# The memory branch of a 1,024-token block: its inputs fetched earlier, its norm beside the last queries, its keys and values at the head of the next stage

## The chip, the core and the metric

One Trainium2 chip, and one of its eight cores. The core has TensorE (PE in the profile; its weight loads are PEld), VectorE (DVE), ScalarE (ACT), GpSimd (POOL) and SyncE (SP), which here only issues transfers. They run side by side and wait for each other through semaphores. The metric is the device time of one execution of the whole program, in microseconds (us).

## What is computed

Two transformer blocks over 1,024 tokens of width 1,024, in fp32. The change touches one part of the first block, the cross attention over a memory of 256 rows:

```python
def _memory_cross_attention(h, mem_n, w_q, w_kv, w_o):
    q = (h @ w_q).reshape(b, s, MEM_HEADS, MEM_HEAD_DIM)                  # 4 heads of 128
    kv = (mem_n @ w_kv).reshape(b, n_mem, 2, MEM_HEADS, MEM_HEAD_DIM)     # 256 rows
    k, v = kv[:, :, 0], kv[:, :, 1]
    sc = jnp.einsum('bshd,bmhd->bhsm', q, k) * MEM_HEAD_DIM ** -0.5
    p = jax.nn.softmax(sc, axis=-1)
    o = jnp.einsum('bhsm,bmhd->bshd', p, v).reshape(b, s, MEM_WIDTH)
    return o @ w_o
```

`h` is the RMS norm of the residual `x` after the first attention has been merged into it, and `mem_n` is the RMS norm of the 256 memory rows with the gain `norm_mem_g`. Nothing else in the program depends on the memory.

## The kernel before

A stage is a Python function that opens a block: each engine gets its own stream of instructions in the order written, and all engines meet at the block's end. Inside it only semaphores order the engines. A tile is 128 tokens; there are eight (ST). A product that matters for precision runs as three fp32r products of a high and a low part (`add_product`, L201 to L203); the memory's keys and values and the scores are plain fp32, each of whose products stands as two records in the trace.

`memory_mixer` (L2240) runs these stages one after the other:

1. `mixed_queries` (L1637) merges the attention output into the residual and makes the queries. Eight chunks of `w_out` are split into the pair `mix_ws` (2 x 4 MB), the weights of `out_rows`. For each tile i the PE does `out_rows(i)` with the previous tile's `turn_out` (eight transposes) in it, then `query(i - 1)`; `turn_query` (four transposes) trails by two. ACT and DVE norm the new residual rows (`norm_out`, `high_out`, `low_out`). The eighth `out_rows` counts `products` to 8, and from there `mix_ws` is read by no one. The queries end up in `qt` (`mem_q`).
2. `load_rows` fetches `mem` (1 MB).
3. `norm_turn` squares the two memory tiles (one on ACT, one on DVE), forms the scale, scales both (ACT), transposes each (PE, eight transposes) and applies the gain column by column (DVE) into `mem_t`.
4. `project_rows` makes the four key heads `km` from four 512 KB loads, two buffers deep.
5. `project_tokens` makes the values `vm` from one 2 MB load.
6. `memory_tiles` (L1974) loads and splits `w_mem_o`, then per tile: `score`, `shift` (row maximum and subtraction, DVE), `exponentials` (ACT), `weigh` (DVE), `turn_probs`, `copy_probs` (ACT), `multiply` by `vm`, `head_high` and `head_low`, and `out_rows` with the pair `cross_ws`. On the PE the order is `score(i)`, `turn_probs(i-1)`, `multiply(i-1)`, `out_rows(i-1)`. A later norm's rows go through `gained` (POOL) to DRAM.

The expert stages follow; they read what `memory_tiles` leaves.

## Time and profile before

| | |
|---|---|
| median of 3 runs | 3433.58 us (3427.8 to 3451.54) |
| the profiled execution, device time | 3434.03 us |
| its span, first to last instruction | 3432.3 us |
| mean granted TensorE clock | 0.958 of full |
| PE busy | 3159.5 us (92%) |
| DVE, ACT, POOL busy | 1610.4, 1411.0, 422.2 us |
| mem_q complete (end of `mixed_queries`) | 754.03 us |
| first `cross_scores` product | 815.82 us |
| third tile's first `cross_scores` product | 839.89 us |

All times below are microseconds from the span's start. A row of the timeline is: start, duration, engine, line, operation, output<-input, shape, how many records (x), and in brackets how long the engine had been idle before it and what released it. A row of a stretch is: from:to, its length, then busy time and number of records (x) of PE, PEld, DVE, ACT and POOL, the granted TensorE clock (PEclk, as a share of 2.4 GHz), the mean busy share of the 16 DMA engines, and GB/s. SPq is a transfer issued by SP; DMA to landing counts from the issue until the data are there.

### The profile page before, as it was taken

What the parts mean: (1) busy time and instruction counts of PE and PEld (TensorE: products, weight loads), DVE (VectorE), ACT (ScalarE), POOL (GpSimd) and SP (SyncE); (2) the same over time, 40 slices, a digit from 0 to 9 for tenths busy, and PEclk for the clock granted to TensorE, in tenths of its full rate; (3) what the DMA queues carried; (4) which work ended last, traced back from release to release, by engine and by line L of the source; (5) the groups of instructions that cost most, each with busy time, mean ns of one, the idle gap of its engine ahead of it and who ended that gap; (6) DMA issues with size and microseconds to landing.
All of it is one profiled execution on the core that took longest, in us unless ns stands there. A gap on an engine that the chain in (4) does not pass through costs nothing. (4 is left out here: it accounts for less than half of the span.)

```text
span 3432.3 us, 39469 instructions
## 1 busy us (share of the span) xinstructions
PE 3159.5 (92%) x15067; PEld 2509.9 (73%) x15067; DVE 1610.4 (47%) x2295; ACT 1411.0 (41%) x2238; POOL 422.2 (12%) x433
## 2 busy tenths in 40 slices
PE   6998998977959999958998999999989889999999
PEld 5767997765847776757776877777777678888787
DVE  4336887323655656552321222332266476565343
ACT  4325777422436666643522333333353333232111
POOL 0001110000122222110000000000000032221332
PEclk9999999998969999979999999999999999999999
DMA  2344231102157777651233222232264222222531
GB/s 86 85 131 112 57 84 60 57 26 81 44 199 285 282 283 272 229 184 44 81 105 102 62 68 68 62 121 83 62 222 137 93 68 82 84 85 82 205 105 53
DMA packets 243195, 397.23 MB, mean 116 GB/s; under 512 B 43575, under 2 KB 162430, under 8 KB 230722
## 3 DMA queue, kind: packets, MB, share of 16 engines
q1 hardware_dynamic: 218386, 346.96, 31.5%
q10 hardware_dynamic: 9072, 30.94, 2.2%
q0 software_dynamic: 15552, 16.82, 1.7%
q8 instruction: 122, 2.00, 0.2%
q14 instruction: 63, 0.52, 0.0%
HBM read 362.41 MB, written 95.65 MB: 133 GB/s over the span
## 5 line engine op out<-in xcount | busy, mean ns | idle before, releaser
L2644 DVE TENSOR_TENSOR moe_wgu_low<-moe_raw,moe_wgu_high 128x2048 fp32r<-128x2048 f32 x94 | 211.2, 2288 | 182.7 <-ACT moe_wgu_high L2601 182.7
L201 PE MATMUL ga_gate<-second_h_high,ga_ws_high 128*128 128x512 f32 x512 | 232.4, 454 | 0.0
L202 PE MATMUL ga_gate<-second_h_low,ga_ws_high 128*128 128x512 f32 x512 | 205.4, 401 | 0.0
L203 PE MATMUL ga_gate<-second_h_high,ga_ws_low 128*128 128x512 f32 x512 | 205.0, 400 | 0.0
L2601 ACT ACTIVATE moe_wgu_high<-moe_raw 128x2048 fp32r<-128x2048 f32 x94 | 174.5, 1906 | 24.3 <-PEq L2275 24.3
L2569 PE MATMUL moe_down<-moe_raw_down,moe_ht 128*128 128x512 f32 x376 | 169.2, 593 | 1.7 <-ACT moe_ht L2634 1.7
L201 PE MATMUL pr_acc<-second_h_high,pr_ws_high 128*128 128x512 f32 x352 | 147.6, 419 | 18.6 <-DVE pr_stage L2946 9.5
L3585 ACT ACTIVATE ga_row<-ga_turned 128x256 f32<-128x256 f32 (+4 forms) x96 | 44.6, 464 | 274.8 <-PE ga_turned L3499 274.8
L201 PE MATMUL moe_up<-moe_wgu_high,moe_xt_high 128*128 128x512 f32 x376 | 152.5, 405 | 4.2 <-DVE moe_xt_low L2650 4.2
L201 PE MATMUL up_bank<-second_h_high,up_w_high 128*128 128x512 f32 x352 | 139.1, 395 | 18.2 <-DVE up_w_low L3180 16.2
L4451 DVE TENSOR_TENSOR second_h_low<-down_hidden,second_h_high 128x1024 fp32r<-128x1024 f32 x42 | 84.7, 2017 | 138.5 <-ACT second_h_high L4426 138.5
L203 PE MATMUL moe_up<-moe_wgu_high,moe_xt_low 128*128 128x512 f32 x376 | 148.5, 395 | 0.0
L202 PE MATMUL moe_up<-moe_wgu_low,moe_xt_high 128*128 128x512 f32 x376 | 148.4, 395 | 0.0
L201 PE MATMUL down_acc<-second_h_high 128*128 128x512 f32 x352 | 138.3, 393 | 7.4 <-DVE second_h_low L4451 7.4
L202 PE MATMUL pr_acc<-second_h_low,pr_ws_high 128*128 128x512 f32 x352 | 141.2, 401 | 0.0
L3489 PE MATMUL ga_scores<-X 64*128 64x256 f32 (+6 forms) x320 | 125.5, 490 | 16.9 <-DMA X<-scratch_fox_k 10.8
L203 PE MATMUL pr_acc<-second_h_high,pr_ws_low 128*128 128x512 f32 x352 | 140.9, 400 | 0.0
L202 PE MATMUL up_bank<-second_h_low,up_w_high 128*128 128x512 f32 x352 | 138.3, 393 | 0.0
L203 PE MATMUL up_bank<-second_h_high,up_w_low 128*128 128x512 f32 x352 | 138.1, 392 | 0.0
L202 PE MATMUL down_acc<-second_h_low,second_h_high 128*128 128x512 f32 x352 | 138.0, 392 | 0.0
L203 PE MATMUL down_acc<-second_h_high,second_h_low 128*128 128x512 f32 x352 | 137.9, 392 | 0.0
L201 PEld LDWEIGHTS ga_gate<-second_h_high,ga_ws_high 128*128 128x128 f32 x512 | 98.6, 193 | 52.9 <-issue 35.1
(581 smaller groups left out, 7833.9 us busy)
## 6 DMA issues: line engine op xcount, KB each, us to landing
moe_raw<-in_w_expert_gate_dram SPq DMA_DIRECT2D x32, 1024.0 KB, 8.5
moe_raw<-in_w_expert_up_dram SPq DMA_DIRECT2D x32, 1024.0 KB, 7.9
moe_raw_down<-in_w_expert_down_dram SPq DMA_DIRECT2D x32, 1024.0 KB, 7.4
scratch_expert_rows<-moe_y ACTq DMA_DIRECT2D x47, 512.0 KB
ga_w<-in_w_in_dram SPq DMA_DIRECT2D x32, 512.0 KB, 4.1
scratch_gates<-ga_stage SPq DMA_DIRECT2D x64, 256.0 KB, 3.6
mb_spare<-scratch_gates SPq DMA_DIRECT2D x32, 512.0 KB, 3.6
up_raw<-in_w_gate_dram SPq DMA_DIRECT2D x22, 512.0 KB, 4.2
```

Source lines behind the costliest of these rows:

```text
L201: nc.tensor.matmul(out, w[0], x[0], start=start, stop=False)
L202: nc.tensor.matmul(out, w[0], x[1], start=False, stop=False)
L203: return nc.tensor.matmul(out, w[1], x[0], start=False, stop=stop)
L2569: last = nc.tensor.matmul(down[:, h * HALF:(h + 1) * HALF], ht[:, c, :], w[:, c, h * HALF:(h + 1) * HALF], start=(c == 0), stop=(c == 1))
L2601: nc.scalar.activation(wgu[i % 2][0][:, :, m, :], raw[(2 * i + m) % RAW][:].rearrange("p (c n) -> p c n", n=FF), ACT.Copy).then_inc(up_hig ...
L2644: nc.vector.tensor_tensor(wgu[i % 2][1][:, :, m, :], raw[(2 * i + m) % RAW][:].rearrange("p (c n) -> p c n", n=FF), wgu[i % 2][0][:, :, m, ...
L3489: last = nc.tensor.matmul(scores[:, at:to], own[0:rows, t * P:(t + 1) * P], other[0:rows, key + at:key + to], start=True, stop=True)
L3585: nc.scalar.activation(pt[:, 0:chunks_of(n), :], turned[:, 0:chunks_of(n), :], ACT.Copy).then_inc(copied, 1)
L4451: nc.vector.tensor_tensor(h_pair[j % 3][1], hidden_of(j), h_pair[j % 3][0], ALU.subtract).then_inc(lows, 1)
```

## The change

The stages 2 to 5 are gone. Their work moves into the two that stay.

- **Space.** The pair `mix_ws` is opened and closed ahead of two tensors `mem_kv` and `mem_rest` of 4 MB each, so that these take its place. `mem_kv` holds `w_mem_kv`; `mem_rest` holds `mem` (1 MB) and `w_mem_o` (2 MB). `mem_t` lies in `gained`.
- **Fetch.** SP, behind its loads of `x`, waits for the eighth `out_rows` (`products` at 8) and then issues `mem`, the four 1 MB parts of `w_mem_kv`, and `w_mem_o`.
- **Norm.** `memory_means` and `memory_gain` (DVE), `memory_scales` (ACT) and `turn_memory` (PE) stand in `mixed_queries` around the last tile's queries. Both memory tiles go through one PSUM tile, `turned_in`, where there were two before.
- **Keys and values.** They open the next stage: `memory_keys` (four heads side by side over the eight chunks), the first tile's `score(0)`, then `memory_values`. ACT copies the keys out in four pieces and the values in one; `score(0)` waits for the keys, `multiply` for the values.

```diff
--- before.py
+++ after.py
-def mixed_queries(k, qt, w, factor, gain):
+def memory_views(W):
+    kv, rest = W
+    return kv, rest[:, 0:2, :], rest[:, 2:6, :]
+
+def mixed_queries(k, qt, mem_t, W, memory, w, factor, gain):
...
+            def turn_memory(t):
+                pe.wait_ge(k.memory_steps["scales"], t + 1)
+                pe.wait_ge(lows_in, ST)
+                if t:
+                    pe.wait_ge(k.memory_steps["gained"], t)
+                for c in range(KD):
+                    last = nc.tensor.transpose(turned_in[:, c, :], rows[t][:, c * P:(c + 1) * P], k.ident[:])
+                last.then_inc(k.memory_steps["turns"], 1)
+
             turn_in(0)
             for i in range(ST + 2):
+                if i == ST + 1:
+                    turn_memory(0)
...
                 if 1 <= i <= ST:
                     query(i - 1)
+            turn_memory(1)
...
+            def memory_scales():
+                step = k.memory_steps
+                act.wait_ge(k.memory_in, 16)
+                act.wait_ge(squares_out, ST)
+                nc.scalar.activation(junk[:], mem[:, 0, :], ACT.Square, accum_out=mem_stats[:, 0, 0:1]).then_inc(step["squares"], 1)
+                act.wait_ge(step["means"], 1)
+                nc.scalar.activation(mem_stats[:, 2, :], mem_stats[:, 1, :], ACT.Sqrt).then_inc(step["roots"], 1)
+                act.wait_ge(step["rstds"], 1)
+                act.wait_ge(turns_in, ST)
+                for t in range(2):
+                    nc.scalar.activation(rows[t][:], mem[:, t, :], ACT.Copy, scale=mem_stats[:, 3, t:t + 1]).then_inc(step["scales"], 1)
...
+                if i == ST + 1:
+                    memory_scales()
                 if i >= 2:
                     query_rows(i - 2)
                     query_cols(i - 2)
...
+            memory_means()
+            memory_gain(0)
+            memory_gain(1)
...
+            sp.wait_ge(products, ST)
+            sp.dma_start(mem, k.dram["mem"].rearrange("a (t p) d -> p (a t) d", p=P)).then_inc(k.memory_in, 16)
+            kv_view = k.dram["w_mem_kv"][0].rearrange("(c p) n -> p c n", p=P)
+            for n in range(4):
+                sp.dma_start(kv[:, 2 * n:2 * n + 2, :], kv_view[:, 2 * n:2 * n + 2, :]).then_inc(k.memory_kv_in[n], 16)
+            sp.dma_start(mem_out, k.dram["w_mem_o"][0].rearrange("(h p) n -> p h n", p=P)).then_inc(k.memory_out_in, 16)
...
+            def memory_keys():
+                pe.wait_ge(k.memory_steps["gained"], 2)
+                for c in range(KD):
+                    pe.wait_ge(k.memory_kv_in[c // 2], 16)
+                    for h in range(MEM_HEADS):
+                        last = nc.tensor.matmul(keys[h], kv[:, c, h * MEM_HD:(h + 1) * MEM_HD], mem_t[:, c, :],
+                                                start=(c == 0), stop=(c == KD - 1))
+                last.then_inc(k_products, 1)
+
+            def memory_values():
+                for c in range(KD):
+                    for t in range(2):
+                        last = nc.tensor.matmul(acc[:, t * MEM_W:(t + 1) * MEM_W], mem_t[:, c, t * P:(t + 1) * P], kv[:, c, MEM_W:],
+                                                start=(c == 0), stop=(c == KD - 1))
+                last.then_inc(v_products, 1)
+
             def score(t):
                 pe.wait_ge(shifted, t)
+                if t == 0:
+                    pe.wait_ge(k_copied, MEM_HEADS)
...
-            for i in range(ST + 3):
+            memory_keys()
+            score(0)
+            memory_values()
+            for i in range(1, ST + 3):
...
+            act.wait_ge(k_products, 1)
+            for h in range(MEM_HEADS):
+                nc.scalar.activation(km[:, h, :], keys[h], ACT.Copy).then_inc(k_copied, 1)
...
                     for c in range(MEM_HEADS):
                         weight(c)
+                    act.wait_ge(v_products, 1)
+                    nc.scalar.activation(vm[:, :, :].rearrange("p c n -> p (c n)"), acc[:], ACT.Copy).then_inc(v_copied, 1)
...
-        with ExitStack() as inner:
-            mem = k.sb("mem_x", [P, MEM_T // P, D], ctx=inner)
-            mem_t = k.sb("mem_t", [P, KD, MEM_T], ctx=inner)
-            load_rows(k, k.dram["mem"].rearrange("a (t p) d -> p (a t) d", p=P), mem)
-            norm_turn(k, "mem_norm", mem, MEM_T // P, k.gain("norm_mem_g"), mem_t)
-            w_kv = k.dram["w_mem_kv"][0]
-            project_rows(k, "mem_k", w_kv[:, 0:MEM_W], MEM_HEADS, mem_t, KD, (km,), tokens=MEM_T)
-            project_tokens(k, "mem_v", [(w_kv[:, MEM_W:].rearrange("(c p) n -> p c n", p=P), 0, MEM_W)],
-                           MEM_W, mem_t, KD, vm, tiles=MEM_T // P)
-        memory_tiles(k, qt, km, vm, logits)
```

On the PE, from the last queries of `mixed_queries` to the first tile of `memory_tiles`, the program had this order (`mix_q_turned` are the last query transposes):

```order
L203 MATMUL mix_q_acc<-mix_wq_high,mix_out_low 128x512
L1744 MATMUL mix_q_turned<-ident,mix_q 128x128 x4
...
L453 MATMUL mem_norm_turned<-ident,mem_norm_scaled 128x128 x16
...
L200 MATMUL mem_k_acc<-mem_t,mem_k_w 128x256 x8
...
L678 MATMUL mem_v_acc<-mem_v_w,mem_v_tokens 128x512 x16
...
L2050 MATMUL cross_scores<-mem_k,mem_q 128x256 x8
```

and has this one after it (`mix_turned_in` now also holds the memory's transposes; `cross_gained` is `mem_t`):

```order
L208 MATMUL mix_q_acc<-mix_wq_high,mix_out_low 128x512
L1750 MATMUL mix_turned_in<-ident,mix_rows 128x128 x8
L1741 MATMUL mix_q_turned<-ident,mix_q 128x128 x4
L1750 MATMUL mix_turned_in<-ident,mix_rows 128x128 x8
...
L2118 MATMUL cross_turned<-cross_gained,mem_kv 128x256 x2
L2118 MATMUL cross_scores<-cross_gained,mem_kv 128x256 x2
...
L2134 MATMUL cross_scores<-mem_k,mem_q 128x256 x4
L2125 MATMUL cross_acc<-mem_kv,cross_gained 128x512 x16
L2134 MATMUL cross_scores<-mem_k,mem_q 128x256 x4
```

The first memory tile's transposes now stand ahead of the last four query transposes, and the 16 value products stand between the first and the second tile's scores. On ACT the memory's square, root and two scalings come ahead of the last query rows, and the key copies open the next stage:

```order
L1841 ACTIVATE mix_junk,mem_stats<-mem_rest 128x1024
L1843 ACTIVATE mem_stats<-mem_stats 128x2
L1847 ACTIVATE mix_rows<-mem_rest,mem_stats 128x1024 x2
L1829 ACTIVATE mix_q<-mix_q_acc 128x512
L1835 ACTIVATE mem_q<-mix_q_turned 128x4x128
...
L2239 ACTIVATE mem_k<-cross_turned 128x256 x2
L2239 ACTIVATE mem_k<-cross_scores 128x256 x2
L2228 ACT_TABLE_LOAD
L2228 ACTIVATE cross_p<-cross_p 128x1024
L2205 ACTIVATE cross_ws_high<-mem_rest 128x1024 x4
L2255 ACTIVATE mem_v<-cross_acc 128x1024
```

So the last query rows wait on ACT behind four new activations, and the value copy stands behind the splitting of `w_mem_o`.

## Rows read from the trace of the kernel before

**Rows 1.** Stretches of 20 us around the memory's stages.
```profile
740.00:760.00 20.00, 9.65 (x48) 7.25 (x46) 1.23 (x1) 3.96 (x6) 0.00 (x0) 0.88 0.16 53
760.00:780.00 20.00, 10.73 (x42) 9.28 (x43) 4.02 (x6) 3.92 (x6) 0.00 (x0) 0.60 0.21 58
780.00:800.00 20.00, 10.24 (x42) 7.78 (x41) 0.00 (x0) 3.15 (x5) 0.00 (x0) 0.82 0.47 153
...
820.00:840.00 20.00, 15.04 (x57) 11.86 (x58) 13.05 (x14) 7.53 (x8) 0.00 (x0) 0.74 0.28 87
```

**Rows 2.** Timeline, the end of `mixed_queries`.
```profile
736.33 1.22 DVE L1907 TENSOR_TENSOR X<-X,mix_acc 128x1024 f32<-128x1024 f32 x1 [3.18 <-PE mix_acc L203]
...
742.91 1.04 PE L1728 MATMUL mix_turned_out<-ident,mix_scaled 128*128 128x128 f32 x8
...
745.04 1.23 DVE L1920 TENSOR_TENSOR mix_out_low<-mix_turned_out,mix_out_high 128x1024 fp32r<-128x1024 f32 x1 [5.68 <-ACT mix_out_high L1814]
...
751.66 0.39 PE L203 MATMUL mix_q_acc<-mix_wq_high,mix_out_low 128*128 128x512 f32 x1
...
753.43 0.60 ACT L1826 ACTIVATE mem_q<-mix_q_turned 128x512 f32<-128x512 f32 x1 [0.75 <-PE mix_q_turned L1744]
```

**Rows 3.** Timeline, load and norm of the memory rows.
```profile
754.28 0.39 SPq L2267 DMA_DIRECT2D mem_x<-in_mem_dram  x1
760.12 1.22 DVE L375 CUSTOM_DVE_ANT_0 mem_norm_junk<-mem_x 128x1024 f32<-128x1024 f32 x1 [13.86 <-PEq L2261]
...
762.11 2.19 ACT L359 ACTIVATE mem_norm_scaled<-mem_x,rstd 128x1024 f32<-128x1024 f32 x2 [0.32 <-DVE rstd L383]
...
767.02 1.23 DVE L390 TENSOR_TENSOR mem_t<-mem_norm_turned,gains 128x1024 f32<-128x1024 f32 x1 [0.48 <-PE mem_norm_turned L453]
```

**Rows 4.** Timeline, the keys and the values.
```profile
772.94 8.59 PE L200 MATMUL mem_k_acc<-mem_t,mem_k_w 128*128 128x256 f32 x32 [5.96 <-DMA mem_k_w<-in_w_mem_kv_dram]
778.22 0.38 ACT L580 ACTIVATE mem_k<-mem_k_acc 128x256 f32 x1 [13.93 <-PE mem_k_acc L200]
...
786.17 0.38 ACT L580 ACTIVATE mem_k<-mem_k_acc 128x256 f32 x1 [4.10 <-PE mem_k_acc L200]
789.63 0.38 ACT L580 ACTIVATE mem_k<-mem_k_acc 128x256 f32 x1 [3.07 <-PE mem_k_acc L200]
...
798.46 16.30 PE L678 MATMUL mem_v_acc<-mem_v_w,mem_v_tokens 128*128 128x512 f32 x32 [8.97 <-DMA mem_v_w<-in_w_mem_kv_dram]
807.94 0.69 DVE L688 COPY mem_v<-mem_v_acc 128x512 f32<-128x512 f32 x1 [39.69 <-PE mem_v_acc L678]
814.80 0.69 DVE L688 COPY mem_v<-mem_v_acc 128x512 f32<-128x512 f32 x1 [6.17 <-PE mem_v_acc L678]
```

**Rows 5.** Timeline of `memory_tiles`: first scores, first two `out_rows`, next scores.
```profile
815.82 1.96 PE L2050 MATMUL cross_scores<-mem_k,mem_q 128*128 128x256 f32 x8 [1.05 <-PEq L634]
...
831.71 0.79 PE L201 MATMUL cross_acc<-cross_ws_high,cross_mixed_high 128*128 128x512 f32 x1 [3.27 <-DVE cross_mixed_low L2195]
...
839.89 1.89 PE L2050 MATMUL cross_scores<-mem_k,mem_q 128*128 128x256 f32 x8
...
847.23 0.50 PE L201 MATMUL cross_acc<-cross_ws_high,cross_mixed_high 128*128 128x512 f32 x1 [1.41 <-DVE cross_mixed_low L2195]
...
852.82 1.89 PE L2050 MATMUL cross_scores<-mem_k,mem_q 128*128 128x256 f32 x8
```

**Rows 6.** Stretches of 2 us: the clock around two pauses and among later transposes.
```profile
744.00:746.00 2.00, 0.00 (x0) 0.00 (x0) 0.96 (x1) 1.00 (x1) 0.00 (x0) 1.00 0.01 4
...
754.00:756.00 2.00, 0.00 (x0) 0.00 (x0) 0.00 (x0) 0.03 (x1) 0.00 (x0) 0.84 0.38 43
...
972.00:974.00 2.00, 2.00 (x12) 2.00 (x11) 0.39 (x2) 0.00 (x0) 0.00 (x0) 0.50 0.00 0
```

**Rows 7.** A 2 us stretch in a burst of nine 1 MB loads.
```profile
954.00:956.00 2.00, 0.00 (x0) 0.00 (x0) 1.79 (x8) 0.21 (x1) 0.00 (x0) 0.50 1.00 426
```

**Rows 8.** Landings of the six `moe_raw` loads among those nine.
```profile
DMA to landing us min/median/max: 5.9/9.9/17.5
```

95 lines of the change are left out of this document (62 added, 33 removed).

## The prediction

> **What bounds the kernel now.** I read the page first: PE is busy 92% of the span, so only places where PE stands still or runs slowly have time to give. The 20 us stretches around the memory's stages show such a place [rows 1]: between 740 and 800 PE is busy for 9.65, 10.73 and 10.24 us of each 20, and the granted clock falls to 0.60 of full. The timeline says what stands there. The last query product ends at 751.66 + 0.39 = 752.05 and the queries are complete at 753.43 + 0.60 = 754.03 [rows 2]. Then `mem` is fetched with nothing else running (issued 754.28, used 760.12) and normed until 767.02 + 1.23 = 768.25 [rows 3]; PE waits 5.96 us for the first key weights and 8.97 us for the value weights [rows 4]; the first scores come at 815.82 [rows 5]. DVE and ACT are nearly idle there [rows 1]. The stretch is a chain: load, norm, load, product, load, product, each alone, with four stage changes between.
>
> The first tile of `memory_tiles` is slow as well: from its `out_rows` at 831.71 to the third tile's scores at 839.89 PE takes 8.18 us, where the second tile takes 852.82 - 847.23 = 5.59 [rows 5]; the clock averages 0.74 in that stretch [rows 1].
>
> **The sum.** I lay the new order along PE with durations from these rows, up to the third tile's scores (839.89 before). Behind them the two programs have the same instructions and waits, so a shift there is carried to the end.
>
> *Fetch.* SP waits for the eighth `out_rows`, which DVE's addition at 736.33 shows as done [rows 2]. All its earlier loads were issued by then (the last `x` tile long before), so nothing is queued ahead. `mem` took 5.84 us from issue to use [rows 3]; in a burst of nine 1 MB loads the earliest landed after 5.9 [rows 8]. So it is there by 736.4 + 5.9 = 742.3. The 16 DMA engines moved 426 GB/s in that burst [rows 7]; `mem` and `w_mem_kv` are 5.24 MB, 12.3 us, so with some 2 us to start the last key weights are there by 751. `w_mem_o` (2.1 MB, 5 us) follows by 756 and isn't asked for before the first scores are through. No other load runs in this time. The transfers cost nothing, and cover is left: the keys want them at 756.9.
>
> *Norm.* DVE's `low_out` ends at 745.04 + 1.23 = 746.27, and ACT is free from 745.0, when `mix_out_high`, which released it, was done [rows 2]. Before, from the start of the DVE square to the end of the first scaling it took 762.11 + 1.1 - 760.12 = 3.1 us, and 4.2 to the second [rows 3]. The same steps here run from 746.3 to 749.4 and 750.5, all under the last query's products, which end at 752.05. The last query rows on ACT, queued behind them, want their product at 752.05 and so lose nothing.
>
> *What stays exposed of it.* `turned_in` is one PSUM tile, so the two memory tiles alternate between PE and DVE. Eight transposes take 1.04 us [rows 2], a gain 1.23 [rows 3]. First transposes 751.9 to 752.95; gain to 754.2; second transposes to 755.3; gain to 756.55. The query transposes and their copy fall between (before, done at 754.03; now some 0.2 later). So the stage ends 2.5 us later than before. A stage change costs 815.82 - (814.80 + 0.69) = 0.33 us [rows 4, 5]. Keys start at 756.9.
>
> *Keys.* Sixteen records at full clock take 789.63 - 786.17 = 3.46 us [rows 4]. There are 64 (32 products): 13.8, and 0.4 until the copy can start: 771.1. Four copies of 0.38 [rows 4] on the path: 772.7.
>
> *score(0)*: 852.82 and 839.89 are starts of such a group; its eight records take 1.7 us at full clock (the group lasts 1.89 with its tail) [rows 5]: 774.4.
>
> *Values*: 32 records, sixteen in 814.80 - 807.94 = 6.86 us [rows 4]: 13.7, to 788.1. Under them lies what used to stand alone in the first tile: the row maximum, the exponentials with their table load, their sum, and the splitting of `w_mem_o`. Before, all of the first tile between its scores and its `out_rows` took 831.71 - 817.78 = 13.9 us, transposes, `multiply` and second scores included [rows 5]; the part that has to be done by 788.1 is shorter than that and has 13.7. The value copy on ACT (1,024 columns out of PSUM, about 1.1 us) runs while PE does score(1).
>
> *First tile.* From a tile's scores to its `out_rows` the second tile took 847.23 - 839.89 = 7.34 us [rows 5]; the same chain stands here: 788.1 + 7.34 = 795.5. `out_rows` at full clock, 5.59: 801.1.
>
> The third tile's scores start at 801.1 in place of 839.89: 38.8 us earlier. The profiled execution took 3434.03, so 3395.2; the median of the runs shown is 0.45 lower: **3394.8, say 3395 us**.
>
> PE's products are the same as before (64 + 32 records of keys and values); what goes is waiting and slow clock. By place: the keys start 772.94 - 756.9 = 16.0 earlier; from there to the last key copy 790.0 - 772.9 = 17.1 becomes 15.8 (1.3); from there to the values 798.46 - 790.0 = 8.4 becomes score(0), 1.7 (6.7); the values 815.8 - 798.5 = 17.4 with a stage change become 13.7 (3.7); the first tile up to its `out_rows` 15.9 becomes 7.3 (8.6); the `out_rows` 8.2 becomes 5.6 (2.6). Sum 38.9, the last digit being rounding.
>
> **The clock.** The forecast takes the high level (2.4 GHz) throughout from 756.9. PE's products pause from 752.05 to 756.9, with 20 transposes in the pause. In the trace products also paused, at least from 742.91 to 746.3, with the eight transposes of 742.91 and four query transposes in the pause, and the clock was 1.00 in 744 to 746 [rows 2, 6]. Behind 752.05, with only four transposes in the pause, it fell: 0.84 on average in 754 to 756 [rows 6]. The new pause is of the first kind. Starting at the low level costs, by rows: the first sixteen key records took 778.22 - 772.94 = 5.28 where 3.46 + 0.4 is full, 1.4 more; the value products took 16.30 where 13.7 is full, 2.6 more [rows 4]; 8.18 against 5.59, again 2.6 [rows 5]. So 1.4 to 2.6 each time the clock has fallen.
>
> The Trainium skill speaks against me here (TensorE: Matmul & The Clock Gate, Part 4: PE-mode transpose): transposes are said not to count as PE work for the clock. By it the new pause is an idle one, the keys would open at 1.2 GHz, and the sum would be that of the first rival. The trace bears it out for the pause behind 752.05 and not for the one before 746.3.
>
> **Rivals.**
> 1. *The clock falls in the pause before the keys, or in the one before the first `out_rows`.* For: it fell behind 752.05, and at 831.71 the first `out_rows` ran slow. Against: the pause at 744, and that the first tile's gaps are now as short as the second tile's (1.41 us before 847.23 [rows 5]), where nothing slowed. Time: 3394.8 + 1.4 to 2.6 = 3396 to 3397.5; both, up to 3400.
> 2. *`mem` lands with the burst behind it.* ACT is in order, so the last query rows would wait behind the memory's square. With `mem` at 751 in place of 742.3 the norm starts 4.7 us later than 746.3, of which 2.4 reach the path (the last product hides the rest), and a longer pause loses the clock too: 38.8 - 2.4 - 2 = 34.4, 3399. Against: the 5.9 of [rows 8].
> 3. *The change doesn't do what it says: the fetch is served only when the stage ends.* Then `mem` is used at 760.1 as before, the norm's alternation ends about 7.7 us after that, and the keys start at 768 at the low clock: 11 + 2 us given back, 3408. Against: `mem` itself was in use 5.84 us after its issue [rows 3], and this issue waits only for a count that is complete at 736.3.
> 4. *Slower than before: the low level stays.* In 972 to 974 PE was busy all of the 2 us and the clock still 0.50 [rows 6]. If it fell at 755 and stayed low through the keys, the values and the first tile, the 39.5 us of full-speed work between 756.9 and 801.1 (13.8 + 1.7 + 13.7 + 7.3 + 5.6, less gaps of 2.6) would double and eat the whole gain; each further tile at the low level, with about 13 us between tiles (852.82 - 839.89 [rows 5]), adds up to 12 and gives 3446. It decides from the end of the first `out_rows` on. Against: in the key and value products the clock came back within their first 16 records each time [rows 4].
>
> **How the numbers follow.** Forecast 0.62; rival 1 0.25; rival 2 0.05; rival 3 0.04; rival 4 0.01; the rest for drift between runs. Low end: the fastest run shown, 3427.8, less 38.8 is 3389; a stage change or pause that is shorter by half a us: 3388. High end: rivals 1 and 2 and the unequal runs, 3405; rival 3 is left out. What a measurement of this kernel can tell from no change is about 1%, 34.3 us, so 3399.2 is the border; forecast and most of rival 1 lie below. Faster by over 1% 0.75, within 1% 0.23, slower 0.02.
>
> **What would show it.** In the profile of the changed kernel: `mem_rest` loaded at 736.4 and used by DVE at 746.3 (rival 2: after 750); the last gain ending near 756.6; the first `cross_turned` product near 756.9 with PEclk 1.00 around it (rival 1: 0.50); key copies near 771.1; values from 774.4 to 788.1; `out_rows` at 795.5; third scores at 801.1. The forecast is wrong if PE waits for a `w_mem_kv` load, if DVE or ACT reaches the first tile's work later than the values' end, or if stages behind 940 lose time that they did not lose before.

## The result, and the profile after

The changed kernel takes 3389.48 us (median of 4 runs, 3387.41 to 3390.73) beside 3434.72 for the kernel before on the same chip: a ratio of 0.9861, 95% interval 0.9825 to 0.9897. Two later comparisons of the same two programs gave 0.9891 (0.9876 to 0.9906) and 0.9889 (0.9873 to 0.9906). The forecast of 3395 us is a ratio of 0.9887 to the 3433.58 us that the prediction started from, and its low end of 3388 one of 0.9867. The 3389.48 us as they stand are inside the range, but they were timed beside a kernel before at 3434.72; put on the prediction's 3433.58 by the ratio they are 3385.9. So the first comparison lies below the forecast range, and the other two are at the forecast.

To read where the time went I cut each profile at two events that all the kernels share. The **first part** runs from the start to the last addition of `mixed_queries` (the row `X<-X,mix_acc`, 736.33 before [rows 2]). The **middle part** runs from there to the third tile's first `cross_scores` (839.89 before [rows 5]). The **last part** is the rest.

| profiled execution | first | middle | last | span |
|---|---|---|---|---|
| before | 736.3 | 103.6 | 2592.4 | 3432.3 |
| changed | 740.8 | 66.3 | 2578.5 | 3385.7 |

The middle part is the change: 37.3 us shorter, where the forecast had 38.8. The 20 us stretches of the changed kernel that answer to [rows 1] show it (columns as there). TensorE is now busy for 16 to 19 of each 20 us, and the 16 DMA engines are nearly full in the first of them (share 0.93).

```profile
740.00:760.00 20.00, 16.46 (x76) 13.06 (x74) 5.15 (x9) 9.18 (x14) 0.00 (x0) 0.91 0.93 360
760.00:780.00 20.00, 16.41 (x78) 14.13 (x79) 1.54 (x2) 2.65 (x6) 0.00 (x0) 1.00 0.18 43
780.00:800.00 20.00, 18.89 (x68) 10.63 (x66) 12.06 (x11) 6.89 (x7) 0.00 (x0) 1.00 0.00 0
800.00:820.00 20.00, 16.06 (x82) 13.32 (x81) 11.62 (x13) 9.18 (x11) 2.42 (x1) 1.00 0.00 1
```

The timeline of the changed kernel, first DVE and SP from the last addition on, then ACT. It answers to [rows 2, 3].

```profile
740.84 0.39 SPq L2014 DMA_DIRECT2D mem_rest<-in_mem_dram  x1
740.84 1.22 DVE L1930 TENSOR_TENSOR X<-X,mix_acc 128x1024 f32<-128x1024 f32 x1 [3.31 <-PE mix_acc L208]
741.27 2.58 SPq L2017 DMA_DIRECT2D mem_kv<-in_w_mem_kv_dram  x4
743.89 0.48 SPq L2018 DMA_DIRECT2D mem_rest<-in_w_mem_o_dram  x1
...
749.56 1.23 DVE L1943 TENSOR_TENSOR mix_out_low<-mix_turned_out,mix_out_high 128x1024 fp32r<-128x1024 f32 x1 [5.69 <-ACT mix_out_high L1823]
750.70 1.22 DVE L1963 CUSTOM_DVE_ANT_0 mix_scaled<-mem_rest 128x1024 f32<-128x1024 f32 x1
...
759.09 1.22 DVE L1973 TENSOR_TENSOR cross_gained<-mix_turned_in,gains 128x1024 f32<-128x1024 f32 x1 [6.53 <-PE mix_turned_in L1750]
761.56 1.22 DVE L1973 TENSOR_TENSOR cross_gained<-mix_turned_in,gains 128x1024 f32<-128x1024 f32 x1 [1.25 <-PE mix_turned_in L1750]
...
752.60 2.19 ACT L1847 ACTIVATE mix_rows<-mem_rest,mem_stats 128x1024 f32<-128x1024 f32 x2 [0.23 <-DVE mem_stats L1969]
...
777.34 0.66 ACT L2239 ACTIVATE mem_k<-cross_turned 128x256 f32<-128x256 f32 x2 [17.19 <-PE cross_scores L2118]
```

DVE starts on `mem` straight behind `mix_out_low`, with no wait for a transfer, and TensorE waits for no load in the whole stretch. TensorE in the same stretch, answering to [rows 4, 5]:

```profile
750.84 0.50 PE L206 MATMUL mix_q_acc<-mix_wq_high,mix_out_high 128*128 128x512 f32 x1 [2.37 <-DVE mix_out_low L1943]
...
757.78 0.40 PE L208 MATMUL mix_q_acc<-mix_wq_high,mix_out_low 128*128 128x512 f32 x1
758.02 1.04 PE L1750 MATMUL mix_turned_in<-ident,mix_rows 128*128 128x128 f32 x8
...
763.26 1.10 PE L2118 MATMUL cross_turned<-cross_gained,mem_kv 128*128 128x256 f32 x4 [1.73 <-PEq L1653]
...
778.70 1.97 PE L2134 MATMUL cross_scores<-mem_k,mem_q 128*128 128x256 f32 x8 [1.39 <-ACT mem_k L2239]
780.50 13.90 PE L2125 MATMUL cross_acc<-mem_kv,cross_gained 128*128 128x512 f32 x32
794.24 1.89 PE L2134 MATMUL cross_scores<-mem_k,mem_q 128*128 128x256 f32 x8
...
801.58 0.50 PE L206 MATMUL cross_acc<-cross_ws_high,cross_mixed_high 128*128 128x512 f32 x1 [1.41 <-DVE cross_mixed_low L2289]
...
807.15 1.89 PE L2134 MATMUL cross_scores<-mem_k,mem_q 128*128 128x256 f32 x8
```

What was not foreseen stands in the 2 us stretches of the last query product. The clock fell there, from 752 until past 755, in a stretch where the kernel before kept it. The last query product took 757.78 + 0.40 - 750.84 = 7.34 us instead of 752.05 - 746.3 = 5.7 [rows 2].

```profile
750.00:752.00 2.00, 1.16 (x5) 0.99 (x6) 1.97 (x4) 0.56 (x2) 0.00 (x0) 1.00 1.02 403
752.00:754.00 2.00, 2.00 (x7) 1.52 (x6) 0.29 (x2) 1.61 (x3) 0.00 (x0) 0.50 1.03 414
754.00:756.00 2.00, 2.00 (x8) 1.61 (x7) 0.00 (x0) 0.78 (x1) 0.00 (x0) 0.64 1.03 410
756.00:758.00 2.00, 2.00 (x10) 1.61 (x9) 0.00 (x0) 0.00 (x0) 0.00 (x0) 1.00 1.02 410
```

### The profile page after: what moved, and what is told of

It reads as the page before. It is cut to its first block and busy times, and to the rows that moved or that the text cites. A ratio compares the mean times of both kernels' runs of the same rounds, so it can differ in the third digit from the quotient of the medians.

```text
span 3385.7 us, 39353 instructions
## 1 busy us (share of the span) xinstructions
PE 3142.6 (93%) x15067; PEld 2500.3 (74%) x15067; DVE 1611.3 (48%) x2293; ACT 1409.4 (42%) x2237; POOL 421.4 (12%) x433
```

## The experiments

All of them in one table. "Excess" is read from the start times of TensorE's records around the merge stage (800 of them): the sum of what the distances from one start to the next between 0.2295 and 0.237 us have above 0.2267 us, the usual distance of these 512-column products; where the 800 begin moves it by some hundredths. "Fall" says whether the clock fell in the last query product, 9 to 12 us behind the addition. Ratios are to the kernel before on the same chip, with their 95% interval; where there is none, the kernel was only profiled. Times in us.

| kernel | ratio | first | middle | last | excess | fall |
|---|---|---|---|---|---|---|
| before | | 736.3 | 103.6 | 2592.4 | 0.61 | no |
| before_again | 0.9999 (0.9985 to 1.0012) | 737.2 | 103.6 | 2586.9 | 0.70 | no |
| changed | 0.9861 (0.9825 to 0.9897) | 740.8 | 66.3 | 2578.5 | 2.03 | yes |
| after_again | 0.9891 (0.9876 to 0.9906) | 739.7 | 66.3 | 2584.4 | 2.01 | yes |
| after_third | 0.9889 (0.9873 to 0.9906) | 737.0 | 66.2 | 2583.6 | 2.11 | yes |
| ws_place | 0.9911 (0.9888 to 0.9933) | 741.0 | 66.3 | 2583.9 | 2.01 | yes |
| late_fetch | 0.9924 (0.9909 to 0.9940) | 738.1 | 76.5 | 2584.1 | 2.05 | yes |
| values_first | | 739.5 | 71.6 | 2584.9 | 1.99 | yes |
| before_pad | | 741.2 | 105.6 | 2592.9 | 2.09 | yes |
| pad_32 | | 737.4 | 105.3 | 2593.5 | 2.00 | yes |
| pad_8192 | | 740.7 | 101.6 | 2591.6 | 0.64 | no |
| stats_last | 0.9877 (0.9862 to 0.9892) | 736.2 | 66.3 | 2588.9 | 0.65 | yes |
| inner_back | 0.9887 (0.9871 to 0.9904) | 759.3 | 64.7 | 2581.5 | 0.62 | no |
| inner_again | 0.9895 (0.9871 to 0.9919) | 736.7 | 66.4 | 2584.7 | 0.64 | yes |
| warm_pause | | 749.9 | 66.4 | 2587.3 | 2.12 | no |
| turns_early | 0.9866 (0.9832 to 0.9900) | 741.9 | 67.2 | 2593.6 | 2.01 | yes |
| turns_warm | 0.9884 (0.9867 to 0.9900) | 738.8 | 63.9 | 2586.4 | 2.14 | no |
| all_three | 0.9905 (0.9887 to 0.9923) | 737.7 | 63.9 | 2584.2 | 0.67 | no |

### Is the gain the middle part, or is there more behind it?

The first profile of the changed kernel had a last part 13.9 us shorter than before, and a ratio beyond the forecast. Theory A: that is chance between executions. Theory B: the change brings something behind its stage. The kernel before was measured again unchanged, and the changed kernel twice.

> The kernel before, unchanged, a second time. I cut an execution in three: up to the last tile's residual addition (736.3 us in the first profile of before), from there to the third tile's first scores (103.6), and from there to the end (2592.4); after the change these were 740.8, 66.3 and 2578.6. The change touches only the middle part, which gave 37.3. Theory A: the 13.8 us gained in the last part come from where the clock happens to fall in an execution, so this second profile has a last part that differs from 2592.4 by several us. Rival B: the last part repeats (within 2 us of 2592.4) and the shift of the stages by the change makes it shorter each time. Both: ratio of the timed runs to before 1.000 within 0.3%, middle part 103.6 within 3.

> The changed kernel, unchanged, with more runs. Theory A: last part anywhere between 2578 and 2592, and a ratio to before near 0.989 (3434 less 38.8). Rival B: last part within 2 us of 2578.6 and a ratio near 0.9865 (46 us). Both: middle part 66 to 68.

> The changed kernel once more, unchanged, beside the kernel before on the same chip. Theory A (the change is worth its middle part, 37 us less 1 to 2 us given back in the merge stage, and what lies beyond this varies from execution to execution): ratio 0.989 with an interval of 0.988 to 0.991, so 35 to 38 us. Theory B (the change brings a further gain behind its own stage, as the first measurement with 0.986 seemed to say): ratio 0.985 to 0.987, 45 to 51 us.

Measured: the kernel before against itself 0.9999, its last part 5.5 us shorter in the second profile than in the first. The changed kernel twice 0.989, its last part 2584.4 and 2583.6 in place of 2578.5. The last part differs by up to 6 us between executions of one program, because the granted clock falls at other places, and of the 13.9 us of the first comparison's profiles 8.1 and 8.8 are left with these two. One such place as the stretches show it, the changed kernel first and its repeat below (0.99 against 0.97 over 200 us at the same work):

```profile
2100.00:2300.00 200.00, 193.56 (x919) 147.18 (x919) 66.52 (x150) 67.83 (x157) 0.00 (x0) 0.99 0.29 87
```
```profile
2100.00:2300.00 200.00, 193.50 (x906) 146.73 (x906) 64.91 (x147) 66.23 (x154) 0.00 (x0) 0.97 0.29 87
```

But theory A isn't all of it. Over all 18 profiles of the table the last part is 2586.9 to 2593.5 us in the five with the old order of stages (mean 2591.5) and 2578.5 to 2593.6 in the thirteen with the new one (mean 2585.1, eleven of them at or below 2587.3). The clock records of the traces have the lower level in the last part for 202 to 218 us in the five (mean 211) and for 188 to 214 in the thirteen (mean 198). So some 6 us of gain lie behind the changed stages on average, and they are clock. The instructions there are the same, and no run here shows how the change reaches the clock that far on.

The first part has the same trait of differing by execution. In the profile of inner_back it took 759.3 us, since the clock was at half for 48 us from 376 on, in a stretch that no variant touches. Below are 20 us of inner_back and then of after_third.

```profile
380.00:400.00 20.00, 20.00 (x86) 18.93 (x85) 10.41 (x25) 10.15 (x25) 0.00 (x0) 0.50 0.00 1
```
```profile
380.00:400.00 20.00, 20.00 (x160) 19.05 (x159) 17.27 (x45) 17.39 (x44) 0.00 (x0) 1.00 0.36 90
```

The profiled execution of inner_back took 3407.25 us, 22 more than its fastest. Several variants have single runs of 3406 to 3415 us, which may be of the same kind; they weren't profiled. Differences of this size are why a ratio of this kernel is uncertain by 0.15 to 0.35%, five to twelve us, while the middle part of a profile repeats to 0.2 us where the clock falls at the same places in it. So steps are judged below by the middle part and by the products' distances.

### The parts of the gain: the early fetch and the order of values and scores

late_fetch issues the same transfers when the stage's queries are all but done:

```diff
-            sp.wait_ge(products, ST)
+            sp.wait_ge(queries, ST)
```

> The changed kernel, but the memory's six loads are issued only when the last query product is done, some 15 us after the last merge product. My theory of the change (a chain of loads and products that stood alone): the memory rows land 5.9 us after the issue, the norm chain starts at 758 instead of 746.3 on the scale of the prediction, and the keys start 9 to 11 us later at a low clock: middle part 66.3 + 11 = 77, ratio to before 0.992. Rival (the early fetch is worth little, the gain is the fewer stages): middle part 66 to 70. The last query rows wait on ScalarE behind the memory's square.

Measured: middle part 76.5, 10.2 longer. The timeline of late_fetch: `mem` issued at 755.46, DVE waits for it until 760.61, and the keys start at 770.68, 32.6 us behind the addition instead of 22.4.

```profile
755.46 0.39 SPq L2014 DMA_DIRECT2D mem_rest<-in_mem_dram  x1
...
760.61 1.23 DVE L1963 CUSTOM_DVE_ANT_0 mix_scaled<-mem_rest 128x1024 f32<-128x1024 f32 x1 [12.56 <-DMA mem_rest<-in_mem_dram]
...
770.68 1.10 PE L2118 MATMUL cross_turned<-cross_gained,mem_kv 128*128 128x256 f32 x4 [1.73 <-PEq L1653]
```

So the early fetch is worth 10 us, and the rest of the 37 comes from joining the stages and from the order. values_first puts `memory_values()` ahead of `score(0)`, so nothing of the first tile lies under the value products:

```diff
             memory_keys()
+            memory_values()
             score(0)
-            memory_values()
```

> The changed kernel with one line moved: score(0) stands behind the value products instead of ahead of them. By the sum of the prediction the first tile's chain (row maximum, exponentials, their sum) then stands alone again: in the kernel before it was 15.9 us from the scores to the out_rows and 8.2 for these at a low clock, in the changed one 7.34 and 5.6. The key copies hide under the values instead (1.2 back). So the middle part (last addition to third tile's scores, 66.3 now) becomes 66.3 - 1.2 + 8.6 - 1.7 = 72, and 74 to 75 if the clock falls again. Rival (the order is indifferent, because the tile's chain waits for the splitting of the output weights anyway): 65 to 67.

Measured: middle part 71.6, 5.3 longer. In its timeline TensorE stands still for 2.57 us behind the first scores, since there is only one tile to work on.

```profile
775.74 13.90 PE L2125 MATMUL cross_acc<-mem_kv,cross_gained 128*128 128x512 f32 x32
789.47 1.89 PE L2134 MATMUL cross_scores<-mem_k,mem_q 128*128 128x256 f32 x8
...
793.94 3.51 PE L2134 MATMUL cross_scores<-mem_k,mem_q 128*128 128x256 f32 x8 [2.57 <-DVE cross_p L2271]
```

### A cost nobody wrote down: the place of the merge stage's tiles

The merge products ran slower in the changed kernel, although no line of them was changed. The cost groups of `mix_acc` over 620 to 736 us show it: the group's three figures are the shortest, middle and longest duration in ns of one product. First the kernel before, then the changed one.

```profile
L201 PE MATMUL mix_acc<-mix_ws_high,mix_in_high x103: 389/389/478, 619.7 to 735.4; 128*128 128x512 f32 x103
```
```profile
L206 PE MATMUL mix_acc<-mix_ws_high,mix_in_high x100: 395/397/483, 619.9 to 735.7; 128*128 128x512 f32 x100
```

What had moved is the place of the tensors in SBUF. I first took the merge weight's place for the cause (ws_place opens `mix_ws` ahead of `gained`, which brings it back to byte 68,896 of the partition), then the tiles behind it (before_pad gives the kernel before one unused tensor of 8,224 bytes per partition, the same shift as in the changed kernel).

```diff
         W = pair(k, "mix_ws", [P, KD, D], ctx)
+        pad = k.sb("mix_pad", [P, 2056], ctx=ctx)
         Q = pair(k, "mix_wq", [P, KD, MEM_W], ctx)
```

> The changed kernel with the merge weight's pair put back at the place in SBUF that it had before the change (the memory's tensors go over it, and mem_t behind them). In the profile after the change the merge's products followed each other in 0.233 us instead of 0.227, while the query products between them kept 0.227. Theory: that is the pair's new place; here the merge's products are back at 0.227 and the stretch from the first full-speed tile to the last addition is about 2 us shorter (384 products by 0.006). Rival: it is the place of the other operand or chance between executions, and the spacing stays at 0.233 or differs without regard to the place. Middle part 66 to 68 in both; whole time 2 us less than the changed kernel by the theory.

> The kernel before with an unused 8,224 bytes per partition between the merge's weights and all other tensors of mixed_queries, so that these stand where the changed kernel has them, and the weights where the kernel before has them. Nothing else is changed. Theory: the merge products' spacing of 0.231 us (median; 0.227 in both profiles of before) comes from the place of the other operand or of the tensors that ScalarE and VectorE use meanwhile, so it is 0.231 here too and the stage 613 to 736 takes 124 us instead of 122.7. Rival: the place has nothing to do with it (something else of the changed program, such as its instruction stream): 0.227.

Measured: ws_place changes nothing (middle 66.3, distance 0.231 us). before_pad makes the products of the kernel before take longer, with an excess of 2.09 us in place of 0.61. It also makes the clock fall in the last query, and the middle part is 105.6 instead of 103.6. Then the way back, in the changed kernel. inner_back allocates the new small tensors behind the tiles, so that `mix_rows`, `mix_in` and `mix_out` are at the old bytes:

```diff
-        mem_stats = k.sb("mem_stats", [P, 4, 2], ctx=ctx)
...
-        square = [k.sb(f"mix_square{n}", [P, DIFF_W], ctx=ctx) for n in range(2)]
-        junk = k.sb("mix_junk", [P, D], ctx=ctx)
         rows = [k.sb(f"mix_rows{n}", [P, D], ctx=ctx) for n in range(2)]
         inner = [pair(k, f"mix_in{n}", [P, KD, P], ctx) for n in range(2)]
         outer = pair(k, "mix_out", [P, KD, P], ctx)
+        square = [k.sb(f"mix_square{n}", [P, DIFF_W], ctx=ctx) for n in range(2)]
+        junk = k.sb("mix_junk", [P, D], ctx=ctx)
+        mem_stats = k.sb("mem_stats", [P, 4, 2], ctx=ctx)
```

> The changed kernel in whole, with the three tensors of the memory norm allocated last, so that the row, input and output tiles of the mixing layers are at the addresses that they have in the kernel before; the merge weight's own tensor stays where the change put it. Theory (the places of the input tiles cost the merge products 0.004 us each): spacing of the merge products back at 0.227 us (0.231 in every run of the changed kind), the stretch of 600 products before the last residual addition 122.7 us instead of 123.5 to 124.4, the first part (start to that addition) 736 to 738 us, the middle part unchanged at 66.3 us, and the whole 1 to 3 us under the changed kernel: a ratio of 0.986 to 0.988 to the kernel before if the last part is at its usual 2,584 to 2,587 us. Rival (the places have nothing to do with it, and the slower spacing comes with some other part of the change): spacing 0.231, stretch 123.5 or more, ratio as for the changed kernel.

Measured: excess 0.62, as before the change. The middle part was 64.7, not the 66.3 that I expected, because the clock did not fall in the last query. The first keys came at 780.09 - 759.28 = 20.81 us behind the addition and the third scores at 64.71 (the forecast: 20.6 and 64.8). Its timeline:

```profile
759.28 1.22 DVE L1930 TENSOR_TENSOR X<-X,mix_acc 128x1024 f32<-128x1024 f32 x1 [3.17 <-PE mix_acc L208]
...
780.09 1.10 PE L2118 MATMUL cross_turned<-cross_gained,mem_kv 128*128 128x256 f32 x4 [1.73 <-PEq L1653]
...
823.99 1.89 PE L2134 MATMUL cross_scores<-mem_k,mem_q 128*128 128x256 f32 x8
```

8,224 is 8,192 + 32, and the 32 are `mem_stats`. Two pads of these sizes on the kernel before (pad_32, then pad_8192, at the same place as in before_pad), and one line moved in the changed kernel (`mem_stats` alone behind `mix_out`), tell them apart; a repeat of inner_back tells whether its clock was chance.

```diff
+        pad = k.sb("mix_pad", [P, 8], ctx=ctx)
...
+        pad = k.sb("mix_pad", [P, 2048], ctx=ctx)
```

> The kernel before with an unused tensor of 32 bytes a partition ahead of the tensors of the merge stage; nothing else is changed. If the odd 32 bytes are what slows the merge products (theory A): 1.8 to 2.1 us above the spacing of 0.2267 in sum, and the clock falls about 10 us behind the last addition, so a middle part of 105 to 106 us. If it is the 8 KB step (theory B): 0.6 to 0.7 us in sum, no fall there, and a middle part of 103.6 us, as in the kernel before.

> The kernel before with an unused tensor of 8,192 bytes a partition ahead of the tensors of the merge stage. Theory A (the odd 32 bytes): as the kernel before, 0.6 to 0.7 us above 0.2267 in sum, a middle part of 103.6 us. Theory B (the 8 KB step, that is which tensors lie past some place in the partition): 1.8 to 2.1 us in sum, the clock falls about 10 us behind the last addition, a middle part of 105 to 106 us.

> The changed kernel with only the 32-byte tensor of the memory's statistics allocated behind the output tiles, so that every tile of the merge stage lies exactly 8,192 bytes further than in the kernel before. Theory A (the odd 32 bytes): 0.6 to 0.7 us above 0.2267 in sum, the clock stays up in the last query, a middle part of 64.7 us. Theory B (the 8 KB step): 2.0 us in sum, the clock falls 10 us behind the addition, a middle part of 66.3 us, as the changed kernel.

> The changed kernel with the tiles of the merge stage at the places that they have in the kernel before, once more. Theory (the places decide both the 1.4 us of slower products and whether the clock falls in the last query): 0.6 to 0.7 us above 0.2267 in sum, no low clock within 30 us of the last addition, a middle part of 64.7 us, as in the one look at it so far. Rival (that the clock stayed up in that look was chance): it falls about 10 us behind the addition, and the middle part is 66.3 us. The ratio would be 0.988 by the first, 0.9885 by the second, which no measurement here tells apart.

Measured: it is the 32 bytes. pad_32 has an excess of 2.00, pad_8192 0.64, stats_last 0.65. The cost groups of pad_32, pad_8192 and stats_last, in this order:

```profile
L201 PE MATMUL mix_acc<-mix_ws_high,mix_in_high x101: 395/397/483, 620.1 to 735.8; 128*128 128x512 f32 x101
```
```profile
L201 PE MATMUL mix_acc<-mix_ws_high,mix_in_high x102: 389/389/628, 619.5 to 735.7; 128*128 128x512 f32 x102
```
```profile
L206 PE MATMUL mix_acc<-mix_ws_high,mix_in_high x102: 389/389/478, 620.3 to 735.3; 128*128 128x512 f32 x102
```

The merge products load `mix_in` as their weights and stream `mix_ws`. In the kernels with products of 389 ns `mix_in0_high` starts at byte 183,584 or 191,776 of the partition, an odd multiple of 32; in those with 395 to 397 ns at 183,616 or 191,808, a multiple of 64. The other three `mix_in` tiles lie 4,096 bytes apart behind it. `mix_ws_high` moves with the change from 68,896 to 77,088, and ws_place and the pads have it at 68,896; so its move isn't the cause, but both are odd multiples of 32, and no run has it at a multiple of 64. So 1.4 us (2.03 - 0.61) of the change's cost is a matter of 32 bytes.

It isn't the start of the weight tile alone. In the changed kernel the query products load `mix_out` (from byte 208,192) and stream `mix_wq` (from 142,656), both at multiples of 64, and they kept the 389 ns that they have before with both at odd multiples of 32. Further on, in both kernels, `pr_acc` and `ga_gate` have their weights at a multiple of 64 and `second_h`, which they stream, at an odd multiple of 32, as the merge products of the changed kernel have, and are as slow as these; `up_bank` has both at odd multiples and isn't. One row of each from the changed kernel, in this order:

```profile
L206 PE MATMUL mix_q_acc<-mix_wq_high,mix_out_high x64: 389/389/632, 628.7 to 757.3; 128*128 128x512 f32 x64
L206 PE MATMUL pr_acc<-second_h_high,pr_ws_high x352: 393/396/802, 1544.5 to 1823.1; 128*128 128x512 f32 x176
L206 PE MATMUL ga_gate<-second_h_high,ga_ws_high x512: 393/397/988, 1834.9 to 2457.6; 128*128 128x512 f32 x171
L206 PE MATMUL up_bank<-second_h_high,up_w_high x352: 387/389/795, 2698.7 to 3132.8; 128*128 128x512 f32 x176
```

So what goes with the longer product is that its two operands start in different halves of 64 bytes. This is read off the kernels as they are: no run moves the streamed operand by 32 bytes, and two groups don't fit (the 512-column products of `twin_scores`, on 96 partitions, take a median of 397 ns or more, and the spare products of the next section 393 to 395, with both operands in the same half).

Both kinds of place are legal by the Trainium skill (SBUF — State Buffer, Operand start alignment): it asks for a multiple of the element's size, four bytes here, and says itself that this is about legality and not speed. In the runs the merge products' pace differs between the two.

As to the clock, the theory fell halfway. In the kernel before it fell in the last query with the tiles at multiples of 64 (2 of 2 profiles: before_pad, pad_32) and not at odd multiples of 32 (0 of 3). In the changed kernel it fell in 7 of 7 profiles with multiples of 64, but also in 2 of 3 with odd multiples of 32. So inner_back's unbroken clock was partly luck, and the places shift the odds at most. The transfers aren't needed for the fall: in pad_32 it came with the DMA engines idle, as this 2 us stretch shows.

```profile
748.00:750.00 2.00, 2.00 (x6) 1.61 (x5) 0.00 (x0) 0.00 (x0) 0.00 (x0) 0.50 0.00 0
```

What the traces do show is a difference in time. In all fifteen profiles with this wait unfilled the clock last rose near the start of the merge stage (between 613 and 639 us), and in the eleven with a fall it fell 133.1 us after that rise, wherever the wait stood. The last addition came 121.8 to 123.4 us behind the rise in these eleven, and 120.5 to 120.9 us behind it in the four without a fall. So the merge stage's 1.4 us are enough to move a kernel from one group into the other, and stats_last and inner_again came as late without them. That this offset in time decides it is argued from the separation: no run shifted the wait on purpose. The 2 us in which the clock rose, in the changed kernel (rise at 618.9, addition at 740.8) and in the one before (615.4 and 736.3):

```profile
618.00:620.00 2.00, 2.00 (x9) 1.60 (x8) 1.17 (x2) 2.00 (x5) 0.00 (x0) 0.78 0.00 0
```
```profile
614.00:616.00 2.00, 2.00 (x7) 1.52 (x7) 0.91 (x3) 0.99 (x3) 0.00 (x0) 0.64 0.03 8
```

The 101.6 of pad_8192 is no gain of the pad. Its clock happened to stay up in the first tile's `out_rows`, which took 5.6 us there and 8.2 in the kernel before.

### The waits in front of the last query and in front of the keys

In the changed kernel TensorE stands still for 2.37 us before the last query product (the row at 750.84), and once more for 0.94 us between the two groups of memory transposes. turns_early moves these transposes into the last query product and gives the second group a PSUM tile of its own. warm_pause puts eight 128x512 products, whose result nobody reads, into the first wait. turns_warm does both (the diff is from it), and all_three is turns_warm with the allocation of inner_back.

```diff
             def query(t):
...
+                if t == ST - 1:
+                    pe.wait_ge(added, ST)
+                    for c in range(KD):
+                        nc.tensor.matmul(acc[:, 0:HALF], inner[1][0][:, c, :], Q[0][:, c, :], start=True, stop=True)
...
+                    if t == ST - 1 and c in (5, 7):
+                        turn_memory(c // 7)
...
-                    last = nc.tensor.transpose(turned_in[:, c, :], rows[t][:, c * P:(c + 1) * P], k.ident[:])
+                    last = nc.tensor.transpose((turned_in, turned_out)[t][:, c, :], rows[t][:, c * P:(c + 1) * P], k.ident[:])
```

> The changed kernel with the memory's transposes in the midst of the last query products (ahead of its 6th and 8th chunk), the second memory tile in the PSUM tile turned_out, so that the two no longer alternate. In the changed kernel the stage ran 4.6 us past the last query product, 4 of them for transposes and gains in alternation. Theory: the stage ends with the last query copy, 2.0 us after the product's end, so the middle part is 66.3 - 2.6 = 63.7 (the transposes cost PE the same 2 us either way). Rival: the scaled memory rows are late (ScalarE), PE waits for them in the products and the middle part is 66 to 68.

Measured: middle part 67.2, where I expected a gain. The transposes take their time (two groups of 1.04 us) inside the query instead of behind it. The keys came 763.46 - 741.90 = 21.6 us behind the addition, 0.9 earlier than in the changed kernel, and the clock fell twice: in the query (0.81 in 752 to 754), and again as the keys began. Below is the timeline, and behind it the 2 us stretch of the keys' start.

```profile
763.46 2.03 PE L2115 MATMUL cross_turned<-cross_gained,mem_kv 128*128 128x256 f32 x4 [1.09 <-PEq L1653]
```
```profile
764.00:766.00 2.00, 2.00 (x6) 1.64 (x5) 0.00 (x0) 0.00 (x0) 0.00 (x0) 0.50 0.82 245
```

> The changed kernel plus eight products of 128x512 (into the merge's accumulator, results unused) in the 2.4 us in which PE waits for the last query's operand. In all three profiles of the changed kernel the granted clock fell shortly after that pause and ten of the last 24 query products ran at 1.2 GHz: they took 7.3 us instead of 5.7. Theory: it is that pause that lets the clock fall; filled, the clock stays 1.00 to the keys and the middle part is 66.3 - 1.6 = 64.7. Rival: the fall has another reason (the fetch of 7 MB at the same time): 66 to 67.

Measured: the products held the clock at 1.00 through the query, which took 5.8 us, but it fell behind the next wait, 0.3 us after the keys had begun, and they ran at the low level (records of 1.73 and 1.91 us where 1.10 and 1.03 are usual). The middle part is the same 66.4. In the timeline and the 2 us stretch of warm_pause:

```profile
770.75 1.73 PE L2122 MATMUL cross_turned<-cross_gained,mem_kv 128*128 128x256 f32 x4 [1.73 <-PEq L1653]
772.27 1.91 PE L2122 MATMUL cross_scores<-cross_gained,mem_kv 128*128 128x256 f32 x4
```
```profile
772.00:774.00 2.00, 2.00 (x7) 1.53 (x6) 0.00 (x0) 0.00 (x0) 0.00 (x0) 0.50 1.10 254
```

> The changed kernel with the transposes of the normed memory inside the last query product, into two buffers, and with eight products that nobody reads (16 half-width ones count as 8 of the full width) at its start, while TensorE would wait for the last addition. Theory (the clock's fall in the last query and the wait for gain copies are each worth 1 to 2 us, and together they can be had): granted clock 1.00 from the addition to the keys' end, the keys begin 19.8 to 20.3 us behind the addition (22.42 in the changed kernel), and the middle part is 63.8 to 64.6 us instead of 66.3. Rival (a stretch of waiting that no longer lets the clock fall in one place lets it fall in the next, as with the products alone): the clock is at its lower level within 8 us of the keys' start, and the middle part is 65.5 to 67 us. By either, the whole lies within 3 us of the changed kernel, less than the last part varies by.

(The spare products are eight of 128x512; the remark on half-width ones in that text is mistaken.) Measured: the keys start 758.77 - 738.77 = 20.00 us behind the addition, the clock is 1.00 throughout, and the middle part is 63.9, its forecast 63.8 to 64.6. The rival, that the fall only moves on, held for warm_pause and not here, where the second wait is gone as well.

> The changed kernel with all that helped one part: the tensors of the memory norm allocated last, the memory's transposes inside the last query product into two buffers, and eight 128x512 products that nobody reads in TensorE's wait for the last addition. If the parts add up (theory): spacing of the merge products at 0.227 us but for some 100 of them, with 0.6 us above 0.2267 in sum in the 800 products before the queries end, where the changed kernel has 2.0; clock 1.00 from the addition to the end of the values; the middle part 63.8 to 64 us; by these two the whole is 1.4 + 2.4 = 3.8 us under the changed kernel, a ratio of 0.9875 to the kernel before. Rival (a saving in one place changes where the clock falls later, and it comes back out in the last part): middle part and spacing as said, last part above 2,588 us, and a ratio of 0.988 to 0.990. Since the last part varied from 2,578 to 2,594 us between runs, the ratio alone may not tell the two apart; the three parts of the profile are what counts.

Measured: the parts add up. Excess 0.67, middle part 63.9, last part 2584.2: by its parts this is the fastest variant, 2.4 us under the changed kernel in the middle and 1.4 in the products. The ratio, 0.9905 (0.9887 to 0.9923), does not show it: two of its six runs lie near 3407. By the ratios no variant of this section can be told from the changed kernel: the lowest of them, 0.9866, is that of turns_early, whose middle part is the longest. Every variant beats the kernel before.

## Why the prediction was right or wrong

**The total.** The forecast of 38.8 us less is a ratio of 0.9887, and both later comparisons (0.9891, 0.9889) have it in the middle of their intervals. The first comparison, 0.9861 of the 3433.58 us, is 3385.9, below the low end of 3388. The step that failed there is that of everything behind the third scores: "Behind them the two programs have the same instructions and waits, so a shift there is carried to the end". It put the change of the last part at nothing, and the range has no term for it either: its low end is "the fastest run shown, 3427.8, less 38.8 is 3389", and half a us. In the profile of the first comparison the last part was 13.9 us shorter than in the one of before, while the first part was 4.5 longer and the middle 37.3 shorter. Of the 13.9, up to 6 is what executions of one program differ by, and the new order of stages has a last part 6.4 us shorter on average, with 13 us less at the lower clock level; why it has, stays open. And a comparison of 4 runs with 4 has an interval of 0.7%, 25 us. The range had to hold that, some 12 us on either side of the forecast, and not 7 below and 10 above for reasons of the mechanism alone. That the later two comparisons met the forecast so closely is in part luck: a middle part 1.5 us short of it, 1.4 us lost ahead, and a gain behind it that it didn't have. On which side of 1% it would fall was right (0.75 for faster by more).

**Fetch: right.** Issued at 740.84 with the addition, as said. The load of `mem` took 5.0 us to land, and the whole burst was through by 760.5, before the keys. The issues in the changed kernel, KB each and median us to landing:

```profile
mem_kv<-in_w_mem_kv_dram SPq DMA_DIRECT2D x4, 1024.0 KB, 10.1
...
mem_rest<-in_mem_dram SPq DMA_DIRECT2D x1, 1024.0 KB, 5.0
```

Rival 2 (`mem` lands with the burst) and rival 3 (fetch served late) did not happen. late_fetch built something like rival 3 and gave 10.2 us back, where that rival's account had 11 + 2.

**Norm under the last query: the mechanism right, its cover mis-sized.** DVE began at 750.70, 9.9 us behind the addition (forecast 10.0). The step that was off is "all under the last query's products, which end at 752.05". The work of these products was taken over from the trace of before at full clock, but the clock fell in them, and the query took 7.34 in place of 5.7, 1.6 more. That is rival 1's price (1.4 to 2.6) at a place that rival 1 did not name: it had the pauses before the keys and before the first `out_rows`. With the clock up, in inner_back, the keys came at 20.8 where the sum had 20.6.

**The alternation and the stage change: nearly right.** From the end of the last query product to the keys it took 763.26 - 758.18 = 5.1 us; the sum had 4.85. The stage change is 0.48 (763.26 - 761.56 - 1.22) and not 0.33.

**Keys, scores, values: right.** Keys to their first copy 777.34 - 763.26 = 14.1 (14.2); to the first scores 1.4, since the copies overlap (1.6); scores 1.8 (1.7); values 794.24 - 780.50 = 13.7 (13.7). The first tile's softmax did fit under the values, and values_first priced that at 5.3 us. From the second tile's scores on: `out_rows` at 801.58, 7.34 behind 794.24 as in the second tile before; 5.57 until the third scores at 807.15 (5.59).

**The clock: right from the keys on, wrong ahead of them.** It stayed at 2.4 GHz from 756 to beyond 810 in the changed kernel, through the pause with 20 transposes in it, so the last-named pause behaved as the forecast said. Of the pause ahead of the last query nothing was foreseen: it has the same twelve transposes and the same 2.4 us of standing still in both kernels, and the clock fell behind it in the one and not in the other. The Trainium skill's rule that transposes don't count as work for the clock (TensorE: Matmul & The Clock Gate, Part 4: PE-mode transpose) fits this better than my reading of [rows 6] did: that pause of 742.91 to 746.3, which I took for proof that transposes keep the clock up, is the very one behind which the clock fell here. Products in the pause kept the clock up in 3 of 3 profiles, transposes did not in 11 of 15. That the clock is sure to fall behind such a pause isn't shown either: it stayed up in the four that are left.

**"PE's products are the same as before": wrong by 1.4 us.** The merge products, whose weight tiles moved from an odd multiple of 32 bytes to a multiple of 64 while the streamed tile stayed at an odd multiple of 32, followed each other after 0.2325 us in place of 0.2284 on average. I counted instructions and waits, and nothing in the diff or in the order of instructions shows a place in memory.

Taken together: 37.3 in the middle less 1.4 ahead of it is 35.9 us, a ratio of 0.9895, and all three measured intervals hold it. The later two ratios, 0.989, are 38 us, and the plain means of all runs on record (3391.1 of 13 runs of the changed kernel, 3432.4 of 58 of the kernel before beside the measurements) are 41 apart. The rest is the shorter last part, whose cause stays open.

**Slower than before (rival 4): no sign.** In the middle part of the changed kernel the low level lasted from 752 until past 755, and never came back.

## What to carry to other kernels

When a fetch and a norm are moved under work that is already there, price each product of the cover at both clock levels, above all behind a wait of TensorE like the one of 2.4 us here, and not only at the level that the old trace happened to show. When a change adds a small tensor, look where it shifts the tiles behind it: allocate small ones last, and compare the middle duration of products that should not have changed. The same comparison finds slow products that were always there: `pr_acc` and `ga_gate`, 2,592 products in either kernel, follow each other after 0.2330 us on average where `up_bank` takes 0.2268. Bringing both operands into the same half of 64 bytes might be worth some 16 us, an estimate from these two figures that no run tests. When a kernel's executions scatter by 0.3%, judge a step by the stretch between two shared events in the profile, compare the stretches behind it over several profiles before they are called chance, and make the range of the total as wide as the comparison itself.

## What the runs showed of the hardware

- **A product's pace can depend on where its operands start within 64 bytes.** With the weight tile at a multiple of 64 and the streamed one at an odd multiple of 32, the 128x512 fp32r products of this stage took 395 to 397 ns and followed each other after 0.2325 us on average; with both at odd multiples of 32 they took 389 ns and 0.2284 us. The query products took 389 ns with both at odd multiples and with both at multiples of 64. Moving the streamed operand alone by 32 bytes was not tried.
- **A small wait can let the clock fall in one execution and not in the next.** The same 2.4 us of standing still, behind the same twelve transposes, was followed by half clock in 11 profiles and by full clock in 4. The fall, where it came, was 133.1 us behind the clock's last rise. Eight spare products in the wait kept the clock up in three profiles; only one of these (warm_pause, addition 122.2 us behind the rise) stands where all without them fell, the other two (123.6 and 121.1) stand outside both groups.
- **One core's load burst ran at 403 to 414 GB/s** from 750 to 758 us beside the query products, and at full clock these kept their distance of 0.227 us.
- **The clock can differ far behind a change.** In the last part, with the same instructions, the lower level took 211 us on average in five profiles with the old order of stages and 198 in thirteen with the new one.
